# Key and value projection: high and low parts of the 64 sample tokens as one stationary operand

## The reference

```
shared = (rmsnorm(x, norm_kv) @ w_kv)      # x: (tokens, 1024), w_kv: (1024, 3072)
# 3072 = 3 groups x (key, value) x 8 heads x 64
rmsnorm(x, g) = x * rsqrt(mean(x*x) + 1e-6) * g
```

## Time and profile before

| | before |
|---|---|
| median of 3 runs | 2506.76 us |
| profiled execution | 2504.07 us |
| its span | 2501.9 us |
| PE busy | 2408.2 us, 96% |
| DVE busy | 1096.6 us, 44% |
| ACT busy | 753.9 us, 30% |
| POOL busy | 254.4 us, 10% |
| kv matmuls L1520, L1521, L1522 | 240 each |
| mean granted TensorE clock | 0.988 |

### The profile page before, as it was taken

How to read it: one execution, slowest core, us unless ns; L and a number is a source line. 1 busy time by engine, 2 the same in 40 slices (tenths; PEclk the granted TensorE clock), 3 DMA queues, 4 the chain that set the end, 5 groups by cost and what they waited for, 6 DMA issues and landing times.

```text
span 2501.9 us, 43531 instructions
## 1 busy us (share of the span) xinstructions
PE 2408.2 (96%) x18470; PEld 2276.1 (91%) x18470; DVE 1096.6 (44%) x1367; ACT 753.9 (30%) x891; POOL 254.4 (10%) x210
## 2 busy tenths in 40 slices
PE   6999999979899999999999999999999989999998
PEld 5999999966599999997778999999977779999997
DVE  5444433577664444332224444433445554444322
ACT  2333321211433333211113333312145533333221
POOL 3000002200130000121000000012001140000021
PEclk9999999999899999999999999999999999999999
DMA  3444522544234445221336444422749822222321
GB/s 112 147 150 150 159 86 74 160 110 102 68 96 144 150 150 161 83 74 59 123 122 208 150 141 150 136 81 68 216 140 265 228 77 84 84 79 82 102 81 38
DMA packets 369898, 306.03 MB, mean 122 GB/s; under 512 B 11015, under 2 KB 334607, under 8 KB 368907
## 3 DMA queue, kind: packets, MB, share of 16 engines
q1 hardware_dynamic: 364635, 237.46, 33.3%
q0 software_dynamic: 5184, 67.43, 7.9%
HBM read 285.51 MB, written 70.54 MB: 142 GB/s over the span
## 4 chain that ended last, share of the span: by engine, by line
PE 91%; DVE 4%; issue 2%; ACT 1%; DMA 0%; SPq 0%; POOL 0%; POOLq 0%; DVEq 0%; ACTq 0%
PE ps L1286 75%; PE ps L1520 2%; PE ps L1521 2%; PE ps L1522 2%; PE ps L1401 1%; PE ps L1557 1%; PE ps L1629 1%; DVE hL L936 1%; PE ps L1605 1%; PE ps L1640 1%; DVE cT L1064 1%; PE ps L1592 1%; PE ps L1575 1%; DVE wL L928 0%; PE ps L1613 0%
## 5 line engine op out<-in xcount | busy, mean ns | idle before, releaser
L928 DVE TENSOR_TENSOR wL<-wst,wH 128x1024 fp32r<-128x1024 f32 (+1 forms) x304 | 423.7, 1394 | 907.4 <-ACT wH L715 906.4
L1286 PE MATMUL ps<-hH,wH 128*128 128x288 f32 x3264 | 704.1, 297 | 17.2 <-DVE hL L936 13.2
L1286 PE MATMUL ps<-hL,wH 128*128 128x288 f32 x3264 | 700.6, 296 | 0.0
L1286 PE MATMUL ps<-hH,wL 128*128 128x288 f32 x3264 | 700.5, 296 | 0.0
L715 ACT CAST wH<-wst 128x1024 fp32r<-128x1024 f32 (+1 forms) x304 | 339.3, 1116 | 1013.9 <-PE ps L1286 847.4
L1286 PEld LDWEIGHTS ps<-hH,wH 128*128 128x128 f32 x3264 | 527.5, 189 | 22.4 <-issue 11.0
L1286 PEld LDWEIGHTS ps<-hL,wH 128*128 128x128 f32 x3264 | 527.6, 189 | 0.0
L1286 PEld LDWEIGHTS ps<-hH,wL 128*128 128x128 f32 x3264 | 527.5, 189 | 0.0
L1286 PE MATMUL ps<-actL,wH 128*128 128x288 f32 x1408 | 301.7, 296 | 0.0
L1286 PE MATMUL ps<-actH,wH 128*128 128x288 f32 x1408 | 301.5, 296 | 0.0
L1286 PE MATMUL ps<-actH,wL 128*128 128x288 f32 x1408 | 301.2, 296 | 0.0
(11 more groups left out here) (198 smaller groups left out, 1957.6 us busy)
## 6 DMA issues: line engine op xcount, KB each, us to landing
wst<-in_ffn_w_in SPq DMA_DIRECT2D x176, 512.0 KB, 3.8
wst<-in_ffn_w_out SPq DMA_DIRECT2D x64, 704.0 KB, 4.6
out_kv_sample<-in_cache_kv_w POOLq DMA_DIRECT2D x8, 4064.0 KB, 15.7
out_kv_sample<-in_cache_kv_w POOLq DMA_DIRECT2D x8, 2016.0 KB, 8.8
wst<-in_conv_w_pw SPq DMA_DIRECT2D x24, 512.0 KB, 4.0
wst<-in_w_kv SPq DMA_DIRECT2D x24, 512.0 KB, 3.6
kc<-in_cache_kv_w SPq DMA_DIRECT2D x40, 256.0 KB
uV<-ucat SPq DMA_DIRECT2D x80, 105.5 KB, 2.2
```

The source lines that it names most:

```text
L928: nc.vector.tensor_tensor(wL[:, s % 2, 0:size], wst[:, s, 0:size], wH[:, s % 2, 0:size].bitcast(f32), ALU.subtract).then_inc(S["w_ready"], 1)
L1286: nx = nc.tensor.matmul(outs[t], a, b[:, t, :], start=start and first, stop=stop and b is xh and not first)
```

## The change

The 64 sample tokens take half of the array's 128 stationary columns. The changed kernel puts their high parts in columns 0 to 63 and their low parts in columns 64 to 127 of a new operand `hS`, and multiplies it by `wH` and by `wL`: two matmuls per slab instead of three. The bank then holds, in partitions 0 to 63, high times both weight parts, and in partitions 64 to 127, low times both weight parts. Low times low, left out before, comes with it. The two halves are added when the bank is emptied: ACT scales the lower half of the partitions' output into `new_low` (partitions 0 to 63 of the buffer `ta`), and DVE's fifth instruction of a group scales the other half and adds it. For this the reciprocal root of the sample tokens is needed on partitions 64 to 127 too, hence one more matmul in `square_sum_tokens`, and one activation and one reciprocal over all five columns in place of two each. The three last are also changed for the last norm.

```diff
+    new_low = ta[0:SMP].rearrange("p a b -> p (a b)")[:, 0:AW]
+    kvst, hS = region(("kvst", [P, 2, TT, AW]), ("hS", [P, KD, P], f32r))
 # ACT, std_tokens
-            nc.scalar.activation(rstdT[:, 0:4], ps[:, 6, 0:4], ACT.Sqrt, scale=1.0 / D, bias=eps[:, 0:1])
-            nc.scalar.activation(rstdT[0:SMP, 4:5], ps[0:SMP, 6, 4:5], ACT.Sqrt, scale=1.0 / D,
-                                 bias=eps[0:SMP, 0:1]).then_inc(S["stdT_ready"], 1)
+            nc.scalar.activation(rstdT[:, 0:TT], ps[:, 6, 0:TT], ACT.Sqrt, scale=1.0 / D, bias=eps[:, 0:1]
+                                 ).then_inc(S["stdT_ready"], 1)
 # ACT, kv
         std_tokens("kv")
+        act.wait_ge(S["h_ready"], HB["kv"] + KD)
+        act.wait_ge(S["pe_chunk"], CB["kv"])
+        nc.scalar.copy(hS[:, :, 0:SMP], hH[:, :, 1, HALF - SMP:HALF].bitcast(f32)).then_inc(S["hs_h"], 1)
+        act.wait_ge(S["kv_evac"], 5)
+        for n in range(6):
             for s in range(4):
+                split_high(CB["kv"] + 4 * n + 2 + s, (s + 2) % 4, SIZE["kv"] if n < 5 or s < 2 else NEXT_SIZE["kv"])
+                if s == 3:
+                    act.wait_ge(S["pe_chunk"], CB["kv"] + 4 * n + 4)
+                    if n:
+                        act.wait_ge(S["kv_evac"], 5 * n + 5)
+                    nc.scalar.mul(new_low, ps[SMP:P, 4, :], rstdT[SMP:P, 4:5]).then_inc(S["kv_low"], 1)
 # DVE, kv
-        me.mark(nc.vector.reciprocal(rstdT[:, 0:4], rstdT[:, 0:4]))
-        nc.vector.reciprocal(rstdT[0:SMP, 4:5], rstdT[0:SMP, 4:5]).then_inc(S["kv_evac"], 5)
-        me.wait()
+        nc.vector.reciprocal(rstdT[:, 0:TT], rstdT[:, 0:TT]).then_inc(S["kv_evac"], 5)
+        dve.wait_ge(S["h_ready"], HB["kv"] + KD)
+        dve.wait_ge(S["pe_chunk"], CB["kv"])
+        nc.vector.tensor_copy(hS[:, :, SMP:P], hL[:, :, 1, HALF - SMP:HALF].bitcast(f32)).then_inc(S["hs_l"], 1)
...
-                    for t in range(TT):
-                        r = P if t < 4 else SMP
-                        nc.vector.tensor_scalar(kvst[0:r, n % 2, t, :], ps[0:r, t, :], rstdT[0:r, t:t + 1], None,
-                                                ALU.mult).then_inc(S["kv_evac"], 1)
+                    for t in range(4):
+                        nc.vector.tensor_scalar(kvst[:, n % 2, t, :], ps[:, t, :], rstdT[:, t:t + 1], None, ALU.mult
+                                                ).then_inc(S["kv_evac"], 1)
+                    dve.wait_ge(S["kv_low"], n + 1)
+                    nc.vector.scalar_tensor_tensor(kvst[0:SMP, n % 2, 4, :], ps[0:SMP, 4, :], rstdT[0:SMP, 4:5],
+                                                   new_low, ALU.mult, ALU.add).then_inc(S["kv_evac"], 1)
 # DVE, last norm: one reciprocal over rstdT[:, 0:TT] in place of two
 # PE, square_sum_tokens
-            nx.then_inc(S["ssT_done"], 1)
+            nc.tensor.matmul(ps[SMP:P, 6, 4:TT], t_[:, SEQ:TOK], ones[:, 0:1], start=True, stop=True
+                             ).then_inc(S["ssT_done"], 1)
 # PE, kv
                     if s == 0:
                         pe.wait_ge(S["kv_evac"], n * 5 + (t + 1))
+                        if t == 4:
+                            pe.wait_ge(S["hs_h"], 1)
+                            pe.wait_ge(S["hs_l"], 1)
                     for k2 in range(2):
                         k = 2 * s + k2
...
+                        if t < 4:
+                            # three matmuls as before, over tokens t * P to (t + 1) * P
+                        else:
+                            both = hS[:, k, :]
+                            nc.tensor.matmul(ps[:, t, :], both, a, start=k == 0, stop=False)
+                            nx = nc.tensor.matmul(ps[:, t, :], both, b, start=False, stop=k == KD - 1)
```

More of the change, by code:

```diff
@@ L238, in trunk_program @@
     assert at[0] <= sb0 + 3 * KD * TOK * 4
-    kvst, = region(("kvst", [P, 2, TT, AW]))
+    new_low = ta[0:SMP].rearrange("p a b -> p (a b)")[:, 0:AW]
+    kvst, hS = region(("kvst", [P, 2, TT, AW]), ("hS", [P, KD, P], f32r))
     qc, qTs, qs, vcA, vcB, kc, kin, vinA, bTA = region(
@@ L303, in trunk_program @@
         state_copy conv_out y_out0 y_out1 w_h w_ready pe_chunk wo_even evac x_ready h_h h_ready
-        sq_ready ss_done std_ready ssT_done stdT_ready silu_done act_in act_h act_ready ident_ready
+        sq_ready ss_done std_ready ssT_done stdT_ready silu_done act_in act_h act_ready kv_low hs_h hs_l ident_ready
         consts_ready par_t par_ready x_t b_mm b_ev sel_ready glu_done st_t st_ready u_ready u_t u_ev
@@ L836, in _ @@
         std_tokens("kv")
-        with act.Fori(0, 5) as i:
-            for s in range(4):
-                split_high(i * 4 + (CB["kv"] + 2 + s), (s + 2) % 4, SIZE["kv"])
-        for s in range(4):
-            split_high(CB["kv"] + 20 + 2 + s, (s + 2) % 4, SIZE["kv"] if s < 2 else NEXT_SIZE["kv"])
+        act.wait_ge(S["h_ready"], HB["kv"] + KD)
[3 more added lines that the diff above has]
+        for n in range(6):
+            for s in range(4):
+                split_high(CB["kv"] + 4 * n + 2 + s, (s + 2) % 4, SIZE["kv"] if n < 5 or s < 2 else NEXT_SIZE["kv"])
[4 more added lines that the diff above has]
+                    nc.scalar.mul(new_low, ps[SMP:P, 4, :], rstdT[SMP:P, 4:5]).then_inc(S["kv_low"], 1)
         act.wait_ge(S["pe_chunk"], CB["ffn2_in"])
@@ L1264, in _ @@
         dve.wait_ge(S["stdT_ready"], 2)
-        me.mark(nc.vector.reciprocal(rstdT[:, 0:4], rstdT[:, 0:4]))
-        me.mark(nc.vector.reciprocal(rstdT[0:SMP, 4:5], rstdT[0:SMP, 4:5]))
+        me.mark(nc.vector.reciprocal(rstdT[:, 0:TT], rstdT[:, 0:TT]))
         me.wait()
-        me.wait(1)
         for t in range(TT):
@@ L1302, in square_sum_tokens @@
                 r = P if t < 4 else SMP
-                nx = nc.tensor.matmul(ps[0:r, 6, t:t + 1], t_[:, t * P:t * P + r], ones[:, 0:1], start=True, stop=True)
-            nx.then_inc(S["ssT_done"], 1)
+                nc.tensor.matmul(ps[0:r, 6, t:t + 1], t_[:, t * P:t * P + r], ones[:, 0:1], start=True, stop=True)
+            nc.tensor.matmul(ps[SMP:P, 6, 4:TT], t_[:, SEQ:TOK], ones[:, 0:1], start=True, stop=True
+                             ).then_inc(S["ssT_done"], 1)
         def in_phase(ph, before_last=None):
@@ L1512, in _ @@
                 for t in range(TT):
-                    r = P if t < 4 else SMP
                     if s == 0:
                         pe.wait_ge(S["kv_evac"], n * 5 + (t + 1))
+                        if t == 4:
+                            pe.wait_ge(S["hs_h"], 1)
+                            pe.wait_ge(S["hs_l"], 1)
                     for k2 in range(2):
                         k = 2 * s + k2
-                        xh, xl = hHf[:, k, t * P:t * P + r], hLf[:, k, t * P:t * P + r]
                         a, b = wH[:, s % 2, k2 * AW:(k2 + 1) * AW], wL[:, s % 2, k2 * AW:(k2 + 1) * AW]
-                        nc.tensor.matmul(ps[0:r, t, :], xh, a, start=k == 0, stop=False)
-                        nc.tensor.matmul(ps[0:r, t, :], xh, b, start=False, stop=False)
-                        nx = nc.tensor.matmul(ps[0:r, t, :], xl, a, start=False, stop=k == KD - 1)
+                        if t < 4:
+                            xh, xl = hHf[:, k, t * P:(t + 1) * P], hLf[:, k, t * P:(t + 1) * P]
+                            nc.tensor.matmul(ps[:, t, :], xh, a, start=k == 0, stop=False)
+                            nc.tensor.matmul(ps[:, t, :], xh, b, start=False, stop=False)
+                            nx = nc.tensor.matmul(ps[:, t, :], xl, a, start=False, stop=k == KD - 1)
+                        else:
+                            both = hS[:, k, :]
+                            nc.tensor.matmul(ps[:, t, :], both, a, start=k == 0, stop=False)
+                            nx = nc.tensor.matmul(ps[:, t, :], both, b, start=False, stop=k == KD - 1)
                 nx.then_inc(S["pe_chunk"], 1)
```

## The result

The changed kernel takes 2492.72 us, the median of 7 runs (2485.11 to 2497.0), against 2505.87 us for the kernel before in the same comparison. The ratio is 0.9943 with a 95% interval from 0.9926 to 0.996, so 10.0 to 18.5 us less. The forecast was 10.45 us less and 2496.3 us. A second comparison gave 2495.31 us (12 runs) against 2506.21 (31 runs, from 2490.63 to 2514.66), ratio 0.9962 (0.9944 to 0.998), so 5.0 to 14.0 us less; between the medians it is 10.9.

The account below looks back on a forecast made before the run. TensorE was taken to bound the key and value projection. Terms -11.0 + 0.2 + 0.1 + 0.25 = -10.45 us, from 2506.76 to a forecast of 2496.3 us, range 2491 to 2502.5.

Parts of the forecast that it names:

- The price of a step and what is removed: Key and value projection: 48 fewer matmuls on TensorE at 0.229 us each, -11.0 us.
- The wider stationary side: Sample tile's weight loads: 128 columns instead of 64 stay hidden beside the running matmul, 0; bounds 0 and +18.3 us.
- The new operand: ACT's and DVE's copies into hS before the stage: about 0.6 us each, over 5 us of slack, so 0.
- The start of the stage: Square sums before the kv stage: sixth matmul +0.39 us, shorter root and reciprocal save some; +0.2, bounds 0 and +0.4.
- The group ends: Five inner kv group borders: the fifth emptying's wait for ACT has 0.8 us of slack and cover behind it, 0.
- The last group's end: Last kv border before ffn2, without cover: DVE's fifth emptying becomes a scalar_tensor_tensor, +0.1 us.
- The last norm: Final norm: the same extra square-sum matmul lies on the path, +0.25 us.
- C: Rival: the sample tile's 96 wider loads are not hidden, up to 0.191 us each, 2514.6 us; chance 0.03.
- D: Rival: ACT and DVE feeding chunks pace the kv stage, PE idles for what it saved, 2507 us; chance 0.03.
- B: Rival: ACT's multiply reaches DVE 1.3 us beyond its slack at the last border, -9.2 or 2497.6 us; chance 0.07.
- A: Rival: three later PE restarts stay at half clock 2.5 us longer, giving back 3.75 us, 2500.1 us; chance 0.09.
- The time: Whole kernel: 10.45 us less, forecast 2496.3 us, 0.42% less.

Follow-up runs that it names:

- experiment 1: Changed kernel with a third matmul per slab put back in the sample tile, all other edits kept: 2504.58 us, ratio 1.0001 to the kernel before.
- experiment 3: Changed kernel with only the 64 high columns of the wide operand used, two matmuls per slab: 2495.41 us, stage 166.59 us.
- experiment 6: Changed kernel with the added square-sum matmul issued first instead of right behind the other 64-column one: 2493.29 us, a single time.
- one_pass: Changed kernel with only one matmul per slab in the sample tile, the product with wL left out: 2486.26 us, stage 155.36 us.
- experiment 5: Changed kernel with two or six more waited multiplies on ACT ahead of the one into new_low at each group end: 2495.73 and 2496.84 us.
- before_again: The kernel before, unchanged, run and profiled once more: 2503.82 us in a single run.
- experiments 3 and 2: Experiment 3, and the changed kernel with only one matmul per slab in the sample tile, the wL product left out: 2486.26 us for the latter.
- narrow_tile: Changed kernel with only the 64 high columns of the wide operand used, low parts of the sample tokens left out: 2495.41 us.
- experiment 8: Changed kernel with unused PSUM banks used at group borders and ACT's and DVE's work reordered at the last group's end: 2489.51 us, ratio 0.9941.
- changed_again: The changed kernel itself, run and profiled once more: 2495.31 us, median of 12.
- three_passes: Changed kernel with a third matmul per slab, a second product with wH, in the sample tile: 2504.58 us, ratio 1.0001 to the kernel before.

## Why the prediction was right

- **The price of a step and what is removed** (-11.0): right, and it is nearly the whole. Groups shrank by 1.87 us; 8 steps of 0.227 are 1.82 (experiment 1 measures 1.81), and the rest is that the wide matmuls of the sample tile step 3 ns to 6 ns shorter than the narrow ones. The prediction took the 48 away at the mean step of 0.229; with its own two steps, 144 x 0.230 less 96 x 0.227, it would have had -11.3. Over the stage, 11.2 measured.
- **The wider stationary side** (0, with 18.3 as the other end): 0 is right, by the sample tile's steps and by experiment 3. The rule of the Trainium skill that was weighed against it ("TensorE: Matmul & The Clock Gate", section "Part 3: Packing small matmuls — row/col tiling") doesn't hold here: loads of 188 ns into all 128 rows fit beside matmuls that step by 227 ns, and loads of 134 ns made the steps no shorter.
- **The new operand** (0): right. The copies take 0.61 and 0.42 us and were done 7 us ahead of use, at 1155.0 against 1162.39.
- **The start of the stage** (+0.2): mis-sized. 2.71 us became 2.59 and 2.76. The term that was too high is the sixth square sum, +0.39 us in the sum: it runs beside the fifth and costs about nothing (experiment 6 shows the 0.37 us where it can't). At equal clock, 0.62 over the first microsecond, the stretch is 2.71 us before and 2.64 in `one_pass`, so the whole term measured -0.07.
- **The group ends** (0): right, and experiment 5 shows the cover as well as its limit.
- **The last group's end** (+0.1): 0.00. The scalar_tensor_tensor takes 733 ns; the tensor_scalar that it replaces took 732.
- **The last norm** (+0.25): not to be seen. It took 2.94 us before and 4.17 after, but 4.20 in the second execution of the kernel before. What differs there is the clock: the mean granted clock of this stretch is 0.77 before and 0.50 in `before_again` and after, so at equal clock the added matmul costs nothing that can be seen.
- **Rivals**: C and D fall by experiments 3 and 2. B is bounded by experiment 5. A is right that low-clock stretches move the time by up to 1.3 us a place from one execution to the next, in both kernels, and that ffn2's restart could lose by it: both executions after ran it 1 us longer at half clock, 0.4 us of time. The 3.75 us of A fell.
- **The time**: the sum, without its +0.55 of small terms, is -11.0 or a little more. The first median, 13.15 lower, lay 3.6 us under the forecast; the second, 10.9 lower, 1.0 under. The difference of those two is scatter and not explained by any step. That the second came so near is in part luck, for the small terms of +0.55 measured about 0, and the 0.4 us at ffn2's restart were in no term.

## What to carry to other kernels

Where TensorE is the bound and a tile fills only half of the stationary columns, two operands that meet the same moving data fit side by side, and each matmul saved was worth its full step here. Adding the halves afterwards cost nothing, because the engines that empty PSUM had slack: work out that slack at an inner border and at the last one separately, since only the last has no cover. Then look at the borders themselves: unused PSUM banks were worth half as much again.

## What the runs showed of the hardware

Two 64-column matmuls into different halves of the output partitions start at the same time (1153.82 in the trace after), so the second is nearly free. The Trainium skill, "TensorE: Matmul & The Clock Gate", section "Part 3: Packing small matmuls — row/col tiling", says that matmuls addressed to different tiles of the array run concurrently, by columns too; the trace agrees.

In two executions (after and `narrow_tile`) the stretch from q's root to the first keys took 68.08 us, in all others 69.65; its matmuls with 288 moving columns then step by 0.131 us on the mean in place of 0.134 (497 and 485 steps in 65 us). What decides between the two wasn't tried and stays open.

A shorter idle time of PE (3.92 us in place of 5.49) didn't keep the clock up (experiment 8). From ffn2's first matmul on, PE ran about 4.4 us at half clock in the kernel before and 5.5 after the change. The stretches of 10 us from that matmul, before, before_again, after and changed_again (the clock is the third number from the end), show 0.78, 0.77, 0.72 and 0.73:

```profile
1333.08:1343.08 10.00, 10.00 (x57) 9.79 (x58) 4.95 (x7) 1.26 (x3) 3.53 (x6) 0.78 0.86 265
1333.16:1343.16 10.00, 9.99 (x56) 9.79 (x57) 4.96 (x7) 1.18 (x3) 3.52 (x6) 0.77 0.88 262
1320.98:1330.98 10.00, 10.00 (x54) 9.79 (x55) 4.96 (x7) 1.76 (x3) 3.52 (x6) 0.72 0.89 269
1321.40:1331.40 10.00, 10.00 (x54) 9.79 (x55) 4.95 (x7) 1.76 (x3) 3.53 (x6) 0.73 0.88 257
```

PE idled 5.49 us ahead of it in all four. The same stretch has 0.70 in `one_pass`, 0.80 in `three_passes` and 0.77 in `narrow_tile`, whose kv stage is as short as that of the changed kernel. The phase that starts there took 0.4 us more in both executions after than in both before. So a part of the change's gain was lost there twice, but whether it must be isn't shown: what sets how long the clock stays low wasn't tried.
